# An encoder's attention heads as one straight program: value products in three f32r passes, another order of ScalarE's and TensorE's steps, scalings on GpSimd

## The chip, the core and the metric

The kernel runs on one core of one Trainium2 chip. The metric is the device time of one execution in microseconds; lower is better.

## What is computed

Two layers of an encoder over 1024 tokens of width 1024. The first mixes with a short gated convolution, the second with multi-head attention over low-rank latents; each is followed by a mixture of 64 experts. The change touches the attention heads alone. Of the reference this is the part:

```python
q = (q_lat @ w_q_up).reshape(b, s, N_HEADS, QK_HEAD_DIM)          # 8 heads, 128 + 64 dims
kv = (kv_lat @ w_kv_up).reshape(b, s, N_HEADS, QK_NOPE_DIM + V_HEAD_DIM)
k_nope, v = kv[..., :QK_NOPE_DIM], kv[..., QK_NOPE_DIM:]
k = concatenate([k_nope, k_rope for every head])
q = rms_norm(q, q_head_norm)
k = rms_norm(k, k_head_norm)
# rope on the last 64 dims of q and k
scores = einsum('bqhd,bkhd->bhqk', qb, k) * scale
probs = softmax(scores, axis=-1)
out = einsum('bhqk,bkhd->bqhd', probs, v)
```

## The kernel before, in words

The program is written engine by engine, each with its own instruction stream; what runs when is set by the order of each stream and by semaphores, with no scheduler between. The phases follow one another: convolution, experts of layer 0, attention, experts of layer 1.

In the attention phase a **tile** is 128 tokens, so a head has NT = 8 tiles, and a **step** s is one tile of queries of one head, 64 steps in all. Two kinds of work are interleaved: step s of a head, and the preparation of tile s + 8, that is of the same tile of the next head.

Preparation of a tile p: `up` (TensorE, L1937 and L1940) multiplies the latents with the head's weights into PSUM bank 4. `squares` (ScalarE, L1616, L1618) sums squares and L1620 copies all 448 columns to `raw`. `find_var` (DVE, L1789, L1792), the power -1/2 (GpSimd, L1548) and `norm_rows` (DVE) follow: L1802 to L1808 scale the rope part of q, the rest of q, k and the shared rope part of k; L1811 to L1815 rotate q. `turn_qk` (TensorE, L1947) turns the four 128x128 pieces into bank 5 or 6, and `split_qk` (DVE, L1825 to L1835) applies the gains and writes a high and a low f32r part of q and of k. GpSimd copies the value columns to `v` (L1553).

Step s: `score` (TensorE, L1959 and L1961) makes 128 x 1024 scores in ten f32r passes of 512 columns: high by high, high by low, low by high, and two for the rope part. `find_max` (DVE, L1839, L1842), `exp` (ScalarE, L1625), `invert` (DVE, L1847), `divide` (ScalarE, L1631). `turn_probs` (TensorE, L1974) turns the probabilities in two groups of four into banks 5 and 6, `copy_probs` (ScalarE, L1639, two instructions) copies them to `probsT`. Each two steps form a pair: `weigh` (TensorE, L1985) multiplies eight tiles of `v` with 256 columns of `probsT`, in plain f32 (each product is two instructions in the trace), and `copy_out` (ScalarE, L1645) stores the 256 columns.

TensorE's order in a step before is `score(s)`, `turn_qk(s+7)`, `up(s+8)`, in odd steps `weigh`, then `turn_probs(s-1)`; the first step of a head differs. ScalarE's is `exp`, `squares`, `divide`, `copy_probs(s-1)`, in odd steps `copy_out`. DVE's is `find_max`, `split_qk`, `invert`, `find_var`, `norm_rows`. The first head and the last are written out, the six between run in a loop of three passes with two heads each. In the last head nothing is prepared any more. SP loads the head's weights, and early in the last head those of the output projection (`sp_load`), which lie over buffers of the projections and of k.

f32r is the type in which a product of f32 values is one pass; a value held as a high and a low f32r part is multiplied in three passes, as `PARTS` says:

```python
HIGH, LOW = 0, 1
PARTS = ((HIGH, HIGH), (HIGH, LOW), (LOW, HIGH))
```

## Time and profile before

| | |
|---|---|
| median of 3 runs | 2750.97 us (2749.24 to 2751.67) |
| the profiled execution | 2754.65 us |
| its span | 2752.9 us |
| TensorE matmul busy | 2357.1 us, 86% |
| DVE, ScalarE, GpSimd busy | 769.6, 644.7, 502.2 us |
| attention heads, first scores to last product | 1329.8 to 1817.2 us |
| DMA moved | 701 MB, 255 GB/s over the span |

The span runs from the first instruction to the last; the execution's own time holds 1.75 us around it. Busy time of an engine is the union of its instructions; TensorE's matmuls are pipelined, so the time from one start to the next is what one costs, and the duration shown for one is longer. PE is TensorE's matmuls, PEld its weight loads, POOL is GpSimd, ACT is ScalarE. In slices of 69 us the DMA engines are busy to 9 tenths in both expert phases and to 0 or 1 in the attention phase.

### The profile page before, as it was taken

The page shows a single profiled execution, that of the slowest core. Times are in us where ns is not written, and L with a number is a line of the kernel's source. Part 1 is how long each engine was busy: PE and PEld are TensorE (multiplying, and loading weights), DVE is VectorE, ACT ScalarE, POOL GpSimd, SP SyncE. Part 2 cuts the span into 40 slices and gives each one's busy share as a digit, 9 for nine tenths or more (in the row PEclk, how much of TensorE's full clock was granted, in tenths as well). Part 3 has the DMA queues.
Part 4 walks back from the last instruction along what each step waited for, and adds up shares of the span by engine and source line. Part 5 has one row for each costly group of instructions (what it writes and reads, how often), then busy time and mean ns, then how long its engine had stood idle before and what let it go on. Part 6 is the DMA issues. An engine that isn't in the chain of part 4 may idle for free. (4 is left out here: it accounts for less than half of the span.)

```text
span 2752.9 us, 35712 instructions
## 1 busy us (share of the span) xinstructions
PE 2357.1 (86%) x12046; PEld 1438.4 (52%) x12046; DVE 769.6 (28%) x2177; ACT 644.7 (23%) x1336; POOL 502.2 (18%) x763
## 2 busy tenths in 40 slices
PE   7999996888888888878899999999598888888883
PEld 5888782333333333357688888768233333333331
DVE  4222342000000000055766666434210000000003
ACT  3111321111111111133455555542111111111111
POOL 2222211212221121211111111011122212222120
PEclk9999997999999999989999999999799999999996
DMA  4111219999999999960000000101899999999997
GB/s 120 48 54 31 77 70 367 423 424 423 423 421 419 418 417 423 389 247 1 9 9 17 8 8 0 61 16 42 355 422 423 424 424 422 422 419 422 416 388 284
DMA packets 136760, 701.17 MB, mean 255 GB/s; under 512 B 36192, under 2 KB 65888, under 8 KB 87536
## 3 DMA queue, kind: packets, MB, share of 16 engines
q1 hardware_dynamic: 116208, 666.65, 59.3%
q0 software_dynamic: 20480, 33.64, 3.2%
q8 instruction: 36, 0.59, 0.1%
q14 instruction: 36, 0.29, 0.0%
HBM read 687.59 MB, written 46.14 MB: 267 GB/s over the span
## 5 line engine op out<-in xcount | busy, mean ns | idle before, releaser
L1337 PE MATMUL ps<-arena 128*64 128x512 f32 x1536 | 445.7, 724 | 207.7 <-issue 109.9
L1318 PE MATMUL ps<-arena 128*64 128x384 f32 x2048 | 348.6, 494 | 2.1 <-DVE arena L1222 2.1
L1337 PEld LDWEIGHTS ps<-arena 128*64 128x64 f32 x1536 | 127.2, 160 | 419.4 <-issue 359.5
L1318 PE MATMUL ps<-gate_up,arena 128*64 128x384 f32 x2048 | 344.4, 489 | 0.0
L1222 DVE TENSOR_TENSOR arena<-ps,xw 128x512 f32<-128x512 f32 x128 | 88.5, 692 | 685.8 <-PE ps L1308 685.8
L843 PE MATMUL ps<-hT_split,w_split 128*128 128x512 f32 x1152 | 265.3, 392 | 3.1 <-DVE hT_split L317 3.1
L843 PEld LDWEIGHTS ps<-hT_split,w_split 128*128 128x128 f32 x1152 | 217.4, 189 | 49.1 <-DVE hT_split L317 3.9
L1231 DVE TENSOR_TENSOR arena<-arena,ps 128x192 f32<-128x192 f32 x128 | 45.4, 354 | 692.5 <-ACT arena L1128 692.5
L1133 ACT ACTIVATE arena<-ps 128x512 f32<-128x512 f32 x128 | 76.5, 597 | 675.8 <-PE ps L1337 665.8
L1318 PEld LDWEIGHTS ps<-arena 128*64 128x64 f32 x2048 | 143.3, 138 | 173.4 <-issue 166.2
L1318 PEld LDWEIGHTS ps<-gate_up,arena 128*64 128x64 f32 x2048 | 141.8, 137 | 168.4 <-issue 159.2
L1122 ACT ACTIVATE arena<-ps 128x384 f32<-128x384 f32 x128 | 62.9, 491 | 628.5 <-PE ps L1318 628.5
L1081 POOL COPY col_idx<-scatter_idx 128x1 int32 (+1 forms) x128 | 23.4, 183 | 956.6 <-ACT arena L1133 896.9
L1074 POOL DMA_INDIRECT arena<-h_rows,col_idx x128 | 134.8, 1053 | 115.6 <-POOL col_idx L1071 108.5
L1084 POOL DMA_INDIRECT y_rows<-arena,col_idx x128 | 131.8, 1030 | 112.9 <-POOL col_idx L1081 112.9
L1985 PE MATMUL ps<-arena 128*128 128x256 f32 x512 | 121.1, 391 | 7.3 <-ACT arena L1639 7.3
L1308 PEld LDWEIGHTS ps<-ident,arena 128*128 128x128 f32 x512 | 71.8, 209 | 100.7 <-issue 100.7
L1328 PEld LDWEIGHTS ps<-ident,arena 128*128 128x128 f32 x384 | 54.8, 202 | 121.0 <-issue 120.1
L1308 PE MATMUL ps<-ident,arena 128*128 128x128 f32 x512 | 96.5, 312 | 25.1 <-DMA arena<-h_rows,col_idx 25.1
L1959 PE MATMUL ps<-k_split,q_split 128*128 128x512 f32 x384 | 114.2, 406 | 0.0
L1985 PEld LDWEIGHTS ps<-arena 128*128 128x128 f32 x512 | 100.4, 197 | 23.3 <-issue 8.7
L1548 POOL TENSOR_TENSOR turned<-turned,minus_half 128x2 f32<-128x2 f32 x64 | 44.6, 698 | 354.7 <-ACT rows L1620 308.7
(218 smaller groups left out, 2926.5 us busy)
## 6 DMA issues: line engine op xcount, KB each, us to landing
arena<-in_exp_w_down SPq DMA_DIRECT2D x128, 1536.0 KB, 19.9
arena<-in_exp_w_gate SPq DMA_DIRECT2D x64, 1536.0 KB, 17.9
arena<-in_exp_w_up SPq DMA_DIRECT2D x64, 1536.0 KB, 26.1
gate_up<-in_exp_w_gate SPq DMA_DIRECT2D x64, 1536.0 KB, 18.5
gate_up<-in_exp_w_up SPq DMA_DIRECT2D x64, 1536.0 KB, 27.0
arena<-in_conv_w_in SPq DMA_DIRECT2D x24, 512.0 KB, 3.8
arena<-y_rows SPq DMA_DIRECT2D x12, 1024.0 KB, 8.2
h_rows<-rows SPq DMA_DIRECT2D x16, 512.0 KB, 2.6
```

Of the source, the lines that this page charges most:

```text
L843: last = pe.matmul(c.ps[:, 3 * h + j, :], w_split[:, j, a, k, :], hT_split[:, b, k, h * BANK:(h + 1) * BANK], start=(k == 0 and a == b), s ...
L1074: pool.indirect_dma_start(gathered[:, slot, :], None, h_halves, bass.IndirectOffsetOnAxis(ap=col_idx[:, slot, :], axis=0), bounds_check=2 ...
L1084: pool.indirect_dma_start(y_halves, bass.IndirectOffsetOnAxis(ap=col_idx[:, 2 + slot, :], axis=0), y[:, slot, :], None, bounds_check=4 * S ...
L1122: act.activation(gate_up[:, slot, :], c.ps[:, 2 + slot, 0:FF], ACT.Copy).then_inc(gate_up_copied, 1)
L1133: act.activation(y[:, slot, :], c.ps[:, 6 + slot, :], ACT.Copy).then_inc(y_copied, 1)
L1222: dve.tensor_tensor(xT[:, slot, :, :, :].rearrange("p j h m -> p (j h) m"), c.ps[:, slot, :].rearrange("p (a m) -> p a m", m=RANKS), bc(c. ...
L1308: last_ = pe.transpose(c.ps[:, slot, j * P:(j + 1) * P], rows[:, j, :], c.ident[:, :])
L1318: last_ = pe.matmul(c.ps[row:row + RANKS, 2 + slot, 0:FF], xT[:, slot, j, half, :], w_gate_up[w_slot][:, i, (4 * half + j) * FF:(4 * half ...
L1328: last_ = pe.transpose(c.ps[:, 4 + slot, j * P:(j + 1) * P], rows[:, j, :], c.ident[:, :])
L1337: last_ = pe.matmul(c.ps[half * RANKS:(half + 1) * RANKS, 6 + slot, :], hidden[:, slot, j, :], w_down[:, slot, j, half * BANK:(half + 1) * ...
L1959: pe.matmul(out, q_split[:, a, 0, q], k_split[:, par, 2 * b, keys], start=(n == 0), stop=False)
L1985: last = pe.matmul(c.ps[:, 7, 0:2 * P], v[:, par, kt, :], probsT[:, j % 2, kt, :], start=(kt == 0), stop=(kt == NT - 1))
```

## The change

1. All 64 steps are written out on every engine; the loops are gone. Slots and buffers come from the step's number.
2. `v` becomes `v_split` and `probsT` a pair of high and low parts, all f32r. GpSimd writes the high part of v with a copy and the low part with a subtraction. ScalarE writes the high part of the turned probabilities (`high_probs`), DVE the low part from the same bank (`low_probs`). `probsT` has one buffer where it had two. `weigh` becomes 24 f32r passes, in two halves of 12, the first (banks' group 0) at the end of an even step, the second after the scores of the odd step.
3. GpSimd scales the rows (L1802 to L1808 before); DVE keeps the rotation (`rotate`), one step later than the variance.
4. The gain of q is multiplied into that of k once; `split_qk` copies q's high part and makes its low part with one instruction.
5. Projections run nine tiles ahead, transposes of q and k eight. TensorE's order is `score(s)`, in odd steps the second half of `weigh`, `turn_probs(s-1)`, `up(s+9)`, in even steps the first half of `weigh`, `turn_qk(s+8)`, always into bank 5.
6. ScalarE: in odd steps `exp(s)`, `copy_out`, `high_probs(s-1)`; in even steps `high_probs(s-1)`, `exp(s)`; then `squares(s+9)`, `divide(s)`.
7. SP waits for the scores of the seventh head too before it loads the output projection's weights. The first scores of a head wait for its k tiles in two halves.

The diff, cut to its core:

```diff
-    v = piece(2, NT, VD)
-    probsT = piece(2, NT, 2 * P)
+    v_split = c.typed("v_split", v_at, [P, 2, 2, NT, VD], F32R)
+    probsT = c.typed("probsT", v_at + 4 * NT * VD, [P, 2, NT, 2 * P], F32R)
...
-    PROB_BANKS = ((5, 6), (6, 5))
+    PROB_BANKS = (5, 6)
+    TILES = NH * NT
+    AHEAD_UP, AHEAD_TURN = NT + 1, NT
...
+            def head_tile(p):
...
+                pool.tensor_tensor(head_rstd[:, slot, :], head_var[:, slot, :], c.minus_half[:, 0:2],
+                                   ALU.pow).then_inc(head_rstd_ready, 1)
+                pool.wait_ge(raw_copied, p + 1)
+                pool.wait_ge(head_rstd_ready, p + 1)
+                wait(pool, qk_turned, p - 1)
+                q_row, k_row, k_rot = (q_k_rows[:, slot, j, :] for j in (0, 2, 3))
+                wait(pool, rot_step, 3 * (p - 1))
+                pool.tensor_scalar(rot[:, 2 + slot, :], raw[:, slot, NOPE:QD], head_rstd[:, slot, 0:1], None,
+                                   ALU.mult).then_inc(rope_scaled, 1)
+                pool.tensor_scalar(q_row, raw[:, slot, 0:NOPE], head_rstd[:, slot, 0:1], None, ALU.mult)
+                pool.tensor_scalar(k_row, raw[:, slot, QD:QD + NOPE], head_rstd[:, slot, 1:2], None, ALU.mult)
+                pool.tensor_scalar(k_rot.rearrange("p (a m) -> p a m", a=2), bc(k_rope[:, i, :], 1, 2),
+                                   head_rstd[:, slot, 1:2], None, ALU.mult).then_inc(rows_scaled, 1)
                 if i == 0:
                     wait(pool, pair_products, 4 * (h - 1))
-                    pool.sem_inc(heads_begun, 1)
-                pool.tensor_copy(v[:, par, i, :], raw[:, i % 2, QD + NOPE:]).then_inc(v_copied, 1)
+                pool.tensor_copy(high, value).then_inc(v_high_ready, 1)
+                pool.wait_ge(v_high_ready, p + 1)
+                pool.tensor_tensor(v_split[:, LOW, h % 2, i, :], value, high, ALU.subtract).then_inc(v_copied, 1)
...
+            for s in range(TILES):
+                if s % 2 == 1:
+                    exp(s)
+                    if s > 1:
+                        copy_out(s // 2 - 1)
+                    high_probs(s - 1)
+                else:
+                    if s > 0:
+                        high_probs(s - 1)
+                    exp(s)
+                if s + AHEAD_UP < TILES:
+                    squares(s + AHEAD_UP)
+                divide(s)
...
-                dve.tensor_tensor(q_high, turned[:, 0:2, :], bc(qk_gain[:, 0:2], 2, P), ALU.mult).then_inc(qk_high_ready, 1)
+                dve.tensor_copy(q_high, turned[:, 0:2, :]).then_inc(qk_high_ready, 1)
...
-                for j in range(2):
-                    dve.scalar_tensor_tensor(out=q_split[:, LOW, j, cols], in0=turned[:, j, :], scalar=qk_gain[:, j:j + 1],
-                                             in1=q_high[:, j, :], op0=ALU.mult, op1=ALU.subtract)
+                dve.tensor_tensor(q_split[:, LOW, :, cols], turned[:, 0:2, :], q_high, ALU.subtract)
...
+            def low_probs(s, g):
+                dve.wait_ge(p_high_ready[g], s + 1)
+                out = slice((s % 2) * P, (s % 2 + 1) * P)
+                dve.tensor_tensor(probsT[:, LOW, 4 * g:4 * g + 4, out],
+                                  c.ps[:, PROB_BANKS[g], :].rearrange("p (a m) -> p a m", m=P),
+                                  probsT[:, HIGH, 4 * g:4 * g + 4, out], ALU.subtract).then_inc(p_low_ready[g], 1)
...
+            for s in range(TILES):
+                find_max(s)
+                if s % 2 == 1:
+                    if s + AHEAD_TURN < TILES:
+                        rotate(s + AHEAD_TURN)
+                    invert(s)
+                    low_probs(s - 1, 0)
+                    low_probs(s - 1, 1)
...
+                if s + AHEAD_TURN < TILES:
+                    split_qk(s + AHEAD_TURN, 5)
+                if s + AHEAD_UP < TILES:
+                    find_var(s + AHEAD_UP)
...
+                for kt in range(4 * part, 4 * part + 4):
+                    for a, b in PARTS:
+                        last = pe.matmul(c.ps[:, 7, 0:2 * P], v_split[:, a, q // 4 % 2, kt, :], probsT[:, b, kt, :],
+                                         start=(kt == 0 and a == b), stop=(kt == NT - 1 and a == LOW))
...
+            for s in range(TILES):
+                score(s)
+                if s % 2 == 1 and s > 1:
+                    weigh(s // 2 - 1, 1)
+                if s > 0:
+                    turn_probs(s - 1, min(s + AHEAD_TURN - 1 + 1, TILES))
+                if s + AHEAD_UP < TILES:
+                    up(s + AHEAD_UP)
+                if s % 2 == 0 and s > 0:
+                    weigh(s // 2 - 1, 0)
+                if s + AHEAD_TURN < TILES:
+                    wait(pe, p_low_ready[0], s)
+                    turn_qk(s + AHEAD_TURN, 5)
```

TensorE's instructions in one pair of steps within the heads, before. Rows stand as issued; `arena` with 256 columns x8 is `weigh`, `arena` with 192 and 256 is `up`, `ident,rows` x8 is `turn_probs`, x4 is `turn_qk`.

```order
L1985 MATMUL ps<-arena 128x256 x8
L1974 MATMUL ps<-ident,rows 128x128 x8
L1959 MATMUL ps<-k_split,q_split 128x512 x3
...
L1961 MATMUL ps<-k_split,q_split 128x512 x2
L1947 MATMUL ps<-ident,rows 128x128 x4
L1937 MATMUL ps<-arena 128x192 x3
L1940 MATMUL ps<-arena 128x256 x2
L1974 MATMUL ps<-ident,rows 128x128 x8
```

The same place with the change: an odd step from its scores on, and the even step after it.

```order
L1957 MATMUL ps<-k_split,q_split 128x512 x2
L1979 MATMUL ps<-probsT,v_split 128x256 x12
L1968 MATMUL ps<-ident,rows 128x128 x8
L1931 MATMUL ps<-arena 128x192 x3
L1934 MATMUL ps<-arena 128x256 x2
L1942 MATMUL ps<-ident,rows 128x128 x4
L1955 MATMUL ps<-k_split,q_split 128x512 x3
...
L1968 MATMUL ps<-ident,rows 128x128 x8
L1931 MATMUL ps<-arena 128x192 x3
L1934 MATMUL ps<-arena 128x256 x2
L1979 MATMUL ps<-probsT,v_split 128x256 x12
```

The transposes of q and k have moved from behind the scores to the end of the step, the transposes of the probabilities from its end to behind the scores, and the value products stand in two places.

ScalarE with the change, an odd step and the even one after it (L1640 is the exponential, L1659 `copy_out`, L1653 `high_probs`, L1630 to L1634 `squares`, L1646 `divide`):

```order
L1640 ACTIVATE rows,turned<-ps,turned 128x1024
L1659 ACTIVATE hT<-ps 128x256
L1653 ACTIVATE probsT<-ps 128x4x128 x2
L1630 ACTIVATE turned<-ps 128x192
L1632 ACTIVATE turned<-ps 128x128
L1634 ACTIVATE rows<-ps 128x448
L1646 ACTIVATE rows<-rows,turned 128x1024
L1653 ACTIVATE probsT<-ps 128x4x128 x2
L1640 ACTIVATE rows,turned<-ps,turned 128x1024
```

Before, the two copies (L1639) stood behind the division in every step; now they stand ahead of the projections' squares, behind the exponential in odd steps and ahead of it in even ones.

## Rows read from the trace of the kernel before

**Rows 1.** Windows: length, busy (instructions) of PE, PEld, DVE, ACT, POOL, clock, DMA, GB/s.

```profile
1397.61:1458.73 61.12, 58.84 (x322) 50.54 (x321) 40.74 (x153) 35.58 (x85) 7.54 (x16) 1.00 0.04 10
...
1582.37:1644.85 62.48, 58.99 (x322) 50.52 (x320) 41.35 (x155) 36.15 (x86) 7.55 (x16) 1.00 0.03 9
...
1764.66:1817.23 52.57, 44.41 (x205) 36.21 (x203) 10.86 (x22) 27.21 (x44) 0.00 (x0) 0.90 0.01 3
```

**Rows 2.** Waits from 1330 to 1780 us: in total, times, longest.

```profile
PE ps L1974 <- DVE k_split L1835: 18.6, 25, 1.5
...
PEld ps L1947 <- DVE rows L1815: 7.5, 18, 0.4
```

**Rows 3.** Timeline of PE, one pair of steps: start, us, what, count [idle before].

```profile
1412.98 3.62 PE L1985 MATMUL ps<-arena 128*128 128x256 f32 x16
1416.44 1.04 PE L1974 MATMUL ps<-ident,rows 128*128 128x128 f32 x8
1417.23 0.94 PE L1959 MATMUL ps<-k_split,q_split 128*128 128x512 f32 x3
...
1419.61 0.60 PE L1947 MATMUL ps<-ident,rows 128*128 128x128 f32 x4
...
1421.89 0.60 PE L1974 MATMUL ps<-ident,rows 128*128 128x128 f32 x4
1423.11 0.63 PE L1974 MATMUL ps<-ident,rows 128*128 128x128 f32 x4 [0.63 <-DVE k_split L1835]
...
1428.37 0.59 PE L1985 MATMUL ps<-arena 128*128 128x256 f32 x2
```

**Rows 4.** Timelines of PE and PEld, and line L329 (min/median/max ns).

```profile
1260.63 0.46 PE L1916 MATMUL ps<-w_lat_high,hT_tile_split 128*128 128x320 f32 x2
1260.92 0.31 PE L1916 MATMUL ps<-w_lat_low,hT_tile_split 128*128 128x320 f32 x1
...
324.60 1.86 PEld L329 LDWEIGHTS ps<-w_router,turned 128*128 128x128 f32 x16
...
L329 PEld LDWEIGHTS ps<-w_router,turned x256: 186/192/192, 324.6 to 1930.6; 128*128 128x128 f32 x128
```

**Rows 5.** Timeline of DVE in the same pair, and L1717 among the groups by line.

```profile
1415.25 0.26 DVE L1802 TENSOR_SCALAR arena<-rows,turned 128x64 f32<-128x64 f32 x1 [0.91 <-POOL turned L1548]
...
1416.13 0.19 DVE L1811 TENSOR_TENSOR arena<-arena,turned 128x32 f32<-128x32 f32 x1
...
1416.59 0.29 DVE L1815 TENSOR_TENSOR rows<-arena 128x128 f32<-128x128 f32 x1
1419.81 1.23 DVE L1839 TENSOR_REDUCE turned<-ps 128x1 f32<-128x1024 f32 x1 [2.93 <-PE ps L1961]
...
1421.14 0.41 DVE L1825 TENSOR_TENSOR q_split<-ps,attn_gain 128x256 fp32r<-128x256 f32 x1
...
L1717 DVE TENSOR_TENSOR hT_tile_split<-ps,hT_tile_split 128x512 fp32r<-128x512 f32 x16 | 10.4, 687 | 13.6 <-ACT hT_tile_split L1571 13.6
```

**Rows 6.** Groups by line on ACT, 1200 to 1800 us: busy, mean ns | idle before.

```profile
L1625 ACT ACTIVATE rows<-ps,turned 128x1024 f32<-128x1024 f32 x62 | 69.1, 1115 | 134.1 <-DVE turned L1842 134.1
...
L1639 ACT ACTIVATE arena<-ps 128x512 f32<-128x512 f32 x122 | 66.9, 604 | 48.1 <-PE ps L1974 48.1
...
L1645 ACT ACTIVATE hT<-ps 128x256 f32 (+1 forms) x30 | 11.7, 389 | 0.0
```

**Rows 7.** Groups by line and shape on POOL, the whole span.

```profile
L713 POOL TENSOR_TENSOR w_split<-arena,w_split 128x1024 fp32r<-128x1024 f32 x24 | 57.4, 2395 | 185.7 <-ACT w_split L740 185.7
L1548 POOL TENSOR_TENSOR turned<-turned,minus_half 128x2 f32<-128x2 f32 x64 | 44.6, 698 | 354.7 <-ACT rows L1620 308.7 <-DVE turned L1792 46.0
...
L1553 POOL COPY arena<-rows 128x128 f32<-128x128 f32 x64 | 18.7, 292 | 57.0 <-PE ps L1985 57.0
```

**Rows 8.** Line L803 on DVE: duration ns min/median/max, first and last start.

```profile
L803 DVE SCALAR_TENSOR_TENSOR rows<-rows,arena x8: 1285/3204/3206, 70.2 to 298.6; 128x1024 f32<-128x1024 f32 x8
```

**Rows 9.** Timeline of PE in the last head.

```profile
1776.76 5.38 PE L1985 MATMUL ps<-arena 128*128 128x256 f32 x16 [2.11 <-ACT arena L1639]
```

More of the change, by code:

```diff
@@ L1564, in _ @@
+                high = v_split[:, HIGH, h % 2, i, :]
+                pool.tensor_copy(high, value).then_inc(v_high_ready, 1)
+                pool.wait_ge(v_high_ready, p + 1)
+                pool.tensor_tensor(v_split[:, LOW, h % 2, i, :], value, high, ALU.subtract).then_inc(v_copied, 1)
+            for p in range(TILES):
+                head_tile(p)
             out_projection.pool_program(pool)
@@ L1664, in _ @@
-            for p in range(NT):
-                squares(p, p % 2)
-            for i in range(NT):
-                step(0, i, 0, first=True)
-            with act.Fori(0, (LAST - 1) // 2) as pair:
-                h = pair * 2 + 1
-                for par in (1, 0):
-                    for i in range(NT):
-                        step(h + (1 - par), i, par)
-            for i in range(NT):
-                step(LAST, i, 1, ends=True)
-            n = NH * NT
-            copy_probs(n - 1, NT - 1, 4 * NH - 1)
@@ new lines, in _ @@
+            for p in range(AHEAD_UP):
+                squares(p)
+            for s in range(TILES):
[11 more added lines that the diff above has]
+                divide(s)
@@ L1868, in _ @@
-            for p in range(NT):
-                find_var(p, p % 2, p)
-                if p >= 1:
-                    split_qk(p - 1, 0, p - 1, 5 + (p - 1) % 2)
-                norm_rows(p, p % 2, p)
-            for i in range(NT):
-                step(0, i, 0, first=True)
-            with dve.Fori(0, (LAST - 1) // 2) as pair:
-                h = pair * 2 + 1
-                for par in (1, 0):
-                    for i in range(NT):
-                        step(h + (1 - par), i, par)
@@ L1883, in _ @@
+            for g in range(2):
+                low_probs(TILES - 1, g)
             dve.wait_ge(router_loaded, 16 * 4)
@@ L2021, in _, with weigh @@
-            for p in range(NT):
-                pe.wait_ge(latT_ready, 2 * p + 2)
-                up(p, 0, p, 0)
+            def weigh(q, part):
+                if part == 0:
+                    pe.wait_ge(v_copied, NT * (q // 4 + 1))
+                    wait(pe, pair_copied, q)
+                pe.wait_ge(p_low_ready[part], 2 * q + 2)
+                for kt in range(4 * part, 4 * part + 4):
+                    for a, b in PARTS:
+                        last = pe.matmul(c.ps[:, 7, 0:2 * P], v_split[:, a, q // 4 % 2, kt, :], probsT[:, b, kt, :],
+                                         start=(kt == 0 and a == b), stop=(kt == NT - 1 and a == LOW))
+                last.then_inc((half_products, pair_products)[part], 1)
@@ L2024, in _ @@
+            for p in range(AHEAD_UP):
+                if p < NT:
+                    pe.wait_ge(latT_ready, 2 * p + 2)
+                up(p)
                 if p == 0:
```

244 lines of the change are left out of this document (88 added, 156 removed).

## The prediction

> **What bounds the kernel now.** I read the windows by stage first. They show that the attention heads are a stretch in which TensorE is busy 58.84 of 61.12 us a head (four pairs of steps, in the even heads of the loop) at full clock, with the other engines at two thirds or less and almost no DMA [rows 1]. The output projection and the second layer's experts only start when it is done, and no load of theirs but that of the projection's weights, early in the last head, runs beside it; so what the heads gain or lose, the whole kernel gains or loses. The same table shows 62.48 us for a head that ends a pass of the loop (1.36 us more), and the last head, where nothing is projected any more, at 52.57 us with a granted clock of 0.90. The waits of TensorE come next: the largest is for DVE's split of q and k at L1835, before the second half of the transposes of the probabilities, 25 times, 18.6 us, and the weight loader stands up to 0.4 us for the normed rows of L1815 [rows 2]. Then the timeline of one pair of steps on TensorE [rows 3], where I take every piece from start to start: value products 1412.98 to 1416.44, 3.46 us; eight transposes 0.79; ten score passes 2.38; transposes of q and k plus the projections of the next head 2.28 (1419.61 to 1421.89); then four transposes at 1421.89, which need 0.4, and the other four only at 1423.11, so 0.8 us of waiting; a second step like the first; the pair is over at 1428.37, 15.39 us. So the heads are TensorE's own work plus about 1 us of waiting a pair.
>
> **Value products (the largest edit).** Before: eight products of 256 columns in plain f32, 16 instructions a pair in 3.46 us, 0.216 us each, which is 0.422 ns a column and pass with two passes an instruction [rows 3]. Now: 24 one-pass f32r instructions of 256 columns. No row has one of 256. The nearest has 320: two of them in 0.29 us (1260.63 to 1260.92), 0.146 us each, where 320 columns at 0.422 ns are 0.135; so an f32r pass costs about 12 ns above its columns, and I take 0.108 + 0.012 = 0.120 us [rows 4]. 24 of them are 2.88 us, **0.57 us less a pair**. Lower end: no extra, 0.108 us, 2.59 us. Upper end: as long as a weight load by itself is shown, 0.19 us, 4.6 us; but the router's 16 loads under passes of only 72 columns, each shown as 0.192 us, take 1.86 us together, (1.86 - 0.19) / 15 = 0.111 us from one to the next [rows 4]; loads overlap, and I stay with 0.120. The Trainium skill ("TensorE: Matmul & The Clock Gate", section "Wait — 56ns, not 53.3ns?") has a warm matmul start every N/2.4 GHz plus about 2.5 ns, whatever its type. By that rule 24 passes take 2.6 us and the heads gain some 8 us more than I say; the f32 rows agree with it, the f32r rows of 320 columns do not, and the rows decide.
>
> **Order on TensorE.** Transposes of the probabilities now come ahead of the projections, transposes of q and k at the end of a step, value products in two halves. The split of q and k then lies under the score passes of the next step (2.38 us against a split that before took from 1421.14 to the release at 1423.11, under 2 us [rows 3, 5]). The 0.8 us of waiting goes, and with it the 0.2 us or so a pair for the rows, which are now ready a step earlier. **Gain 1.0 us a pair.**
>
> **The wait that is new.** Transposes of q and k write bank 5 and so wait for DVE's low part of the probabilities of the step before. In an odd step, counted from the last score pass: DVE starts its maximum 0.20 us later (1419.61 to 1419.81), has handed over 1.4 us after that (its next large instruction starts at 1421.14), ScalarE's exponential takes 1.12, the copy of the sums 0.39, the first high half 0.60, DVE's low half 0.69 [rows 5, 6]: 4.4 us. TensorE has half of the value products (1.44), eight transposes (0.79) and the projections (1.84) in between, 4.1 us. With the hand-overs that is a wait of **0.4 us in every odd step**. In an even step the high half goes ahead of the exponential, and the low half is done by about 2.5 us, with no wait. So a pair: 15.39 - 0.57 - 1.0 + 0.4 = 14.2 us.
>
> **At each head's first step** there are two more. The scores' second half wants the k tile that was turned just before: turned, split (some 1.7 us, since one gain goes out of it) and handed over, it comes about 0.8 us after the first half's 1.15 us. And GpSimd's first value tile of a head waits until the head before last has been weighed, which now is two steps later, holding the next tile's power behind it on its queue (it waited there before too, but with nothing behind it that the current step wanted); I take 0.65 us. So a head is 4 x 14.2 + 1.45 = 58.3 us against 61.12: **2.8 us a head**, 19.6 us over the seven heads that project.
>
> **DVE.** Four scalings of rows go to GpSimd (from 1415.25 to 1416.13, 0.9 us a step), one split instruction of two goes; four low halves a pair come, 2.8 us [rows 5]. Its load stays about two thirds of TensorE's span; costed in the chain above, nothing besides. **GpSimd** gets four scalings, a cast and a subtraction a tile. Copies of 128 columns take 0.29 us, the power 0.70, a subtraction of 1024 columns 2.40, thus about 0.3 to 0.45 for 128 [rows 7]; no row shows a scaling there. Between 2.2 us and, at twice that, 4.5 us a tile, in a step of 7.1 us and with a whole step between the projection and the use: nothing, as long as it stays under a step. **ScalarE** has the same instructions in another order. **SP** gets one wait, for the scores of the seventh head, which are there within a step. **The loops** go on every engine: twice 1.36 us, 2.8 us. Straight code loads more instructions; no row shows what that costs, and between nothing and the same 2.8 us again I take nothing, since the first head was straight code before. **Start:** nine tiles are projected ahead for eight, but one fewer projection stands before the first scores; nothing. **Last head:** the gaps of 2.1 us before the value products become two shorter ones; before, three products there took 5.38 us each for 3.62 at the lower clock (1.2 GHz in part) [rows 3, 9]. Nothing on balance, with 5 us of gain if the clock stays up, 2 us of loss from the low halves in the chain if not.
>
> **Sum.** 19.6 + 2.8 = 22 us. The profiled execution took 2754.65 us, so 2732 to 2733 in its terms; the median of the runs shown is 2750.97, 3.7 us below it, and 22 off that is **2729 us**. Lower ends together (0.108 us a pass, of which the chain of the odd step gives back a part, 6 us; the last head's 5): 2718.
>
> **Rivals.**
> (A) *Weight loads set the pace of the value products.* 24 loads for 16, each under a pass half as long. At 0.19 us a pass the pair is 1.1 us longer in the products instead of 0.57 shorter: 14.2 + 1.7 = 15.9 us, a head 65 us, 7 x 3.9 - 2.8, and the kernel about 25 us **slower, 2775**. It decides from 0.149 us a pass on (22 us over 32 x 24 passes above 0.120). For it: loads are shown as 0.19 us. Against: the router's start every 0.111 us [rows 4].
> (B) *DVE and GpSimd get in each other's way.* DVE's sum at L803 takes 1.285 us alone and 3.204 where GpSimd subtracts at the same time [rows 8]. The rotation (four instructions with two operands in SBUF, 0.75 us) and the low halves would be stretched so while GpSimd works on the next tile; with 0.7 us more in both chains of a pair (half of what the rotation could be stretched by, once a step) the gain falls to about 3 us, 2748. That is a rule of the skill too ("GPSIMD Engine Reference", section "Key points": contention with Vector instructions that have two SBUF inputs); the trace agrees for instructions of 1024 columns and shows none for short ones. Against: DVE idles a third of the time, and the power of 0.70 us runs beside it already.
> (C) *The order gives nothing.* The 1.0 us of waiting turns up elsewhere in the ring of score, maximum, exponential, division, transposes. Then only 32 x 0.57 and the loops are left, less 1.45 a head: 18 + 2.8 - 10, 11 us, 2740.
>
> **Chances.** Forecast 0.63, with its own range 2718 to 2736; A 0.10; B 0.12; C 0.15. The range has to take in C and B and leaves A and the tail below out: 2717 to 2748. A measurement of this kernel can tell about 0.2% (5.5 us) from no change. Faster: the forecast, C and a little of B, 0.80. Same: most of B, 0.09. Slower: A and a worse B, 0.11.
>
> **What would show it.** Value products at about 0.12 us from start to start, 1.44 us a half; pairs of 14.2 us, with a longer third and fourth; no wait of transposes on L1835's successor but one of the q and k transposes on the low halves, about 0.4 us in odd steps; heads of 58 us; 22 us less before the output projection and nothing after it. Wrong it is if passes start 0.15 us apart or more, if the rotation takes over 1 us, or if DVE waits for GpSimd's scaling in every step.

## The result, and the profile after

The changed kernel takes **2728.88 us** in the median of four runs (2726.91 to 2731.35), the kernel before beside it 2751.32 us (2749.24 to 2754.48): a ratio of 0.9919, 95% interval 0.9907 to 0.993. The forecast was 2729, and the outcome is the likeliest case of the prediction. The profiled execution took 2731.35 us, 23.3 less than the one before:

| stretch | before | after | difference |
|---|---|---|---|
| up to the end of the latents | 1280.3 | 1279.8 | -0.5 |
| start: to the first scores | 49.5 | 53.2 | +3.7 |
| first scores to last product | 487.4 | 464.7 | -22.7 |
| output projection and experts | 935.7 | 931.9 | -3.8 |

The last row is code that the change doesn't touch, and it varies by itself: 931.9 us here and 934.3 in the second trace of the same kernel (run 1), 931.1 to 935.1 over all traces with the new heads. The windows of the trace (columns as in [rows 1]) show the start, two heads, and the last head in two parts:

```profile
1279.80:1332.98 53.18, 29.96 (x135) 24.62 (x133) 26.72 (x103) 13.12 (x53) 30.80 (x59) 0.78 0.04 11
1455.10:1513.67 58.57, 56.21 (x355) 50.12 (x353) 44.05 (x129) 35.94 (x85) 29.19 (x56) 1.00 0.04 11
1513.67:1572.20 58.53, 56.17 (x355) 50.05 (x353) 44.03 (x128) 35.88 (x85) 29.14 (x56) 1.00 0.03 10
...
1689.26:1747.66 58.40, 52.88 (x335) 46.84 (x333) 43.57 (x125) 34.63 (x80) 26.21 (x51) 1.00 0.16 57
1747.66:1797.70 50.04, 41.81 (x254) 36.49 (x254) 21.44 (x39) 26.69 (x44) 0.00 (x0) 0.93 0.05 20
```

A head is 58.55 us for 61.12 and 62.48 [rows 1], every head alike now, and GpSimd (fifth engine column) is busy 29 us in it for 7.5. The last stretch is 50.04 us for 52.57, at a granted clock of 0.93 for 0.90. A plain pair on TensorE (timeline: start, duration, line, count, idle before):

```profile
1426.09 1.78 PE L1979 MATMUL ps<-probsT,v_split 128*128 128x256 f32 x12
1427.70 0.60 PE L1942 MATMUL ps<-ident,rows 128*128 128x128 f32 x4
1428.06 0.94 PE L1955 MATMUL ps<-k_split,q_split 128*128 128x512 f32 x3
...
1430.44 1.60 PE L1979 MATMUL ps<-probsT,v_split 128*128 128x256 f32 x12
1431.87 1.04 PE L1968 MATMUL ps<-ident,rows 128*128 128x128 f32 x8
1432.74 1.14 PE L1931 MATMUL ps<-arena 128*128 128x192 f32 x6
1433.72 1.03 PE L1934 MATMUL ps<-arena 128*128 128x256 f32 x4
1434.83 0.66 PE L1942 MATMUL ps<-ident,rows 128*128 128x128 f32 x4
...
1438.51 1.14 PE L1931 MATMUL ps<-arena 128*128 128x192 f32 x6
1439.48 1.03 PE L1934 MATMUL ps<-arena 128*128 128x256 f32 x4
1440.16 1.06 PE L1979 MATMUL ps<-probsT,v_split 128*128 128x256 f32 x6
```

The pair is 14.07 us (1426.09 to 1440.16) for 15.39 [rows 3]. Twelve f32r passes take 1.43 us (1430.44 to 1431.87), 0.119 each. From the projection's second part to the transposes of q and k it is 1.11 us (1433.72 to 1434.83); the four products need 0.86 of it, so 0.25 us is a wait. The waits from 1320 to 1790 us (total, times, longest), against [rows 2]:

```profile
POOL v_split L1573 <- PE ps L1979: 37.8, 6, 6.3
...
PEld ps L1942 <- DVE probsT L1837: 24.8, 28, 2.2
...
PE ps L1942 <- POOL rows L1567: 9.1, 6, 1.5
...
PE ps L1955 <- DVE k_split L1823: 5.3, 8, 1.2
```

The 18.6 us for the split before the transposes of the probabilities are gone. The transposes of q and k (L1942) wait for DVE's low half (L1837) in every odd step, and at the second step of six heads for GpSimd's rows; the first scores of a head (L1955) wait for the k tile's split. GpSimd at such a head's beginning:

```profile
1454.19 0.60 POOL L1567 TENSOR_SCALAR rows<-turned 128x128 f32<-128x128 f32 x1
1461.11 0.29 POOL L1573 CAST v_split<-rows 128x128 fp32r<-128x128 f32 x1 [6.31 <-PE ps L1979]
1461.49 0.46 POOL L1575 TENSOR_TENSOR v_split<-rows,v_split 128x128 fp32r<-128x128 f32 x1
1461.91 0.72 POOL L1556 TENSOR_TENSOR turned<-turned,minus_half 128x2 f32<-128x2 f32 x1
...
1464.53 0.60 POOL L1567 TENSOR_SCALAR rows<-turned 128x128 f32<-128x128 f32 x1
```

It stands 6.31 us before the cast of the head's first value tile, and the next tile's rows, due behind it, come at 1465.1; TensorE's transposes start at 1465.28, after 1.52 us of idling.

### The profile page after: what moved, and what is told of

The parts are those of the page before. It is cut to its first block and busy times, and to the rows that moved or that the text cites. A ratio compares the mean times of both kernels' runs of the same rounds, so it can differ in the third digit from the quotient of the medians.

```text
span 2729.6 us, 35801 instructions
## 1 busy us (share of the span) xinstructions
PE 2336.9 (86%) x12300; PEld 1437.3 (53%) x12302; DVE 794.8 (29%) x1986; ACT 645.8 (24%) x1336; POOL 674.7 (25%) x1083
## 5 line engine op out<-in xcount | busy, mean ns | idle before, releaser
L1955 PE MATMUL ps<-k_split,q_split 128*128 128x512 f32 x384 | 115.9, 410 | 5.3 <-DVE k_split L1823 5.3
L1979 PE MATMUL ps<-probsT,v_split 128*128 128x256 f32 x768 | 109.6, 293 | 5.6 <-DVE probsT L1837 5.6
L1979 PEld LDWEIGHTS ps<-probsT,v_split 128*128 128x128 f32 x768 | 102.3, 194 | 10.4 <-issue 6.6
L713 POOL TENSOR_TENSOR w_split<-arena,w_split 128x1024 fp32r<-128x1024 f32 x24 | 57.4, 2395 | 185.8 <-ACT w_split L740 185.8
```

The source lines that it names most:

```text
L1955: pe.matmul(out, q_split[:, a, 0, q], k_split[:, h % 2, 2 * b, keys], start=(n == 0), stop=False)
L1979: last = pe.matmul(c.ps[:, 7, 0:2 * P], v_split[:, a, q // 4 % 2, kt, :], probsT[:, b, kt, :], start=(kt == 0 and a == b), stop=(kt == NT ...
```

## Experiments

Twelve kernels ran, each an edit of the changed kernel unless it says otherwise. All ratios are against the kernel before on the same chip. Differences between runs in microseconds are of medians, in part from different chips, on which the kernel before took 2750.9 to 2753.2 us; what is said of heads, pairs and starts is read from one trace of each kernel.

**1. The change again.**

> The changed kernel once more, untouched, as the measure for the others of this group. 0.992 of the kernel before, 2729 us, whichever theory holds; pairs of steps of 14.07, 14.07, 14.9 and 15.5 us in a head of 58.5.

2728.96 us (2724.93 to 2730.35), 0.991 (0.9895 to 0.9924). It reproduces, and shows what varies: from the first tile's projection to the first scores it is 50.3 us here (1280.57 to 1330.86) and 52.6 in the first profile of the change. The six products of 192 columns, 1.14 us at full clock (2.4 GHz) and 2.13 at half (1.2 GHz), tell why:

```profile
1302.43 1.30 PE L1931 MATMUL ps<-arena 128*128 128x192 f32 x6
...
1308.20 2.08 PE L1931 MATMUL ps<-arena 128*128 128x192 f32 x6
...
1313.50 1.14 PE L1931 MATMUL ps<-arena 128*128 128x192 f32 x6
...
1317.86 1.14 PE L1931 MATMUL ps<-arena 128*128 128x192 f32 x6
```

A tile is 4.36 us at full clock (1313.50 to 1317.86) and 5.3 to 6.6 where the clock is at half for part of it. Of the executions with the order of the change's own start, the profiled ones of runs 2, 4, 5 and 8 have one such tile and need 48.0 us, this one has three, the first profile and run 6 have four (52.6 and 52.5). Differences of up to 4.6 us between two traces are that; below, starts and heads are told apart for it.

**2. Value products in plain f32.**

```diff
-                    for a, b in PARTS:
-                        last = pe.matmul(..., v_split[:, a, q // 4 % 2, kt, :], probsT[:, b, kt, :], ...)
+                    last = pe.matmul(..., v[:, q // 4 % 2, kt, :], probsT[:, kt, :], ...)
```

with `low_probs` and the low value tile gone, and every wait for a low half turned into one for the high half.

> The changed kernel with its value products in plain f32 again (8 products of 256 columns a pair in place of 24 f32r passes), so DVE has no low halves to make and GpSimd only copies the value tile; the order of the work is kept. My theory: the products take 0.57 us a pair longer (3.46 for 2.88), but the wait of the q and k transposes in odd steps goes, since they now wait for ScalarE's high half alone; in the trace of the change that wait is about 0.25 us of TensorE and the second half-step is otherwise full. So pairs of 14.07 + 0.57 - 0.25 = 14.4 us, about 28 x 0.32 = 9 us slower than the change, plus some 3 in the last head: 2741, 0.996 of before. Rival 1, the passes are worth their full 0.57 a pair and DVE's low halves cost nothing (something else would hold TensorE in the odd step): 16 to 18 us slower, 2746. Rival 2, the low halves cost as much as the passes save (DVE's 2.8 us a pair also delays the split or the maximum): same as the change within 3 us.

2730.74 us, 0.9922 (0.991 to 0.9934): **in this order the f32r passes, the prediction's largest edit, are worth 1.8 us** in the median, which the two intervals don't separate from nothing. The window of one head, starts of the value products as its ends:

```profile
1406.31:1465.78 59.47, 57.89 (x322) 50.63 (x321) 34.66 (x112) 35.91 (x86) 25.12 (x48) 1.00 0.04 10
```

A plain pair is 14.34 us for 14.06, so 0.28 slower and not 0.57: the wait for the low half is gone with the low half, as my theory had it, and seven heads lose 6.4 us. The total is nearer to Rival 2, for two reasons outside the pairs: its start is 2.3 us shorter by the clock (48.0 for 50.3), which is no merit of the edit, and the last head's pairs, which have no projections to cover a low half, take 10.74 us for 11.15. From the first scores to the last product it takes 465.06 us for 462.06, so with equal starts the passes are worth 3 to 4 us. The fourth pair of a head hides them too: it is 15.5 us with either, since GpSimd's rows hold it.

**3. The scalings back on DVE.**

```diff
             def rotate(p):
+                dve.wait_ge(raw_copied, p + 1)
+                dve.wait_ge(head_rstd_ready, p + 1)
+                dve.tensor_scalar(rot[:, 2 + slot, :], raw[:, slot, NOPE:QD], ...)
...
```

> The changed kernel with the four scalings of a tile (2.2 us on GpSimd, 0.9 on DVE in the trace of before) back on DVE, ahead of its rotation; the rest untouched. My theory: in the heads DVE stands idle 0.5 us ahead of the low halves of an odd step and 0.5 us more ahead of them after its reciprocal, so 0.9 us more is covered there, and the heads stay at 58.5 within 0.5; the first scores, which came at 1332.98 for 1329.8 before, come 3 to 4 us earlier again, since a tile of the start no longer goes through GpSimd's 2.2 us; so 3 to 4 us faster than the change, 2725. Also the wait of the q and k transposes on GpSimd's rows at a head's second step (1.5 us, six times) shrinks, since the stalled value tile no longer holds the next tile's rows: up to 1.3 us a head, 2717 to 2725. Rival, what the prediction set at nothing is worth something: the 0.9 us lie in the chain from maximum to the low half of an odd step, q and k transposes wait 0.4 us longer in each of 28 pairs, 7 to 11 us slower than the change, 2738.

2746.21 us, 0.9976 (0.9968 to 0.9985): 17 us slower than the change. My theory was right for the heads, which stay within 0.5 us (plain pairs 14.06, a head 58.75), and the rival fell, since odd steps wait no longer than before. But no time is gained: the wait at a head's second step doesn't shrink (that pair is 15.68 us for 15.47), since the power still stands behind the stalled value tile, and the start, where I expected 3 to 4 us of gain, loses most of the time: 61.9 us from the first projection to the first scores (1281.84 to 1343.77) for 50.3, or 48.0 at best. Rows of its timeline, all engines:

```profile
1303.37 2.13 PE L1932 MATMUL ps<-arena 128*128 128x192 f32 x6
1305.29 1.20 PE L1935 MATMUL ps<-arena 128*128 128x256 f32 x4
...
1307.44 0.17 DVE L1785 TENSOR_SCALAR turned<-turned 128x2 f32<-128x2 f32 x1
1307.55 0.25 DVE L1795 TENSOR_SCALAR arena<-rows,turned 128x64 f32<-128x64 f32 x1
...
1308.76 0.29 DVE L1807 TENSOR_TENSOR rows<-arena 128x128 f32<-128x128 f32 x1
...
1309.15 1.09 PE L1943 MATMUL ps<-ident,rows 128*128 128x128 f32 x4 [2.66 <-DVE rows L1807]
...
1310.03 2.13 PE L1932 MATMUL ps<-arena 128*128 128x192 f32 x6
```

DVE takes the new tile's variance (L1785) first, which waits for that tile's projection and its squares, and only then the scalings and the rotation of the tile before; TensorE waits for these and projects no further tile. One turn is 6.66 us. Six products of 192 columns take 2.13 us, where they take 1.14 at full clock: TensorE idles 2.66 us of each turn, and in each of seven tiles running it was back at 1.2 GHz when it began, and near 2.4 GHz again in the tile's last products (1.05 to 1.39 us for 1.03); the granted clock over the last six of these turns is 0.75. In the change the scalings run on GpSimd beside the ring, a turn is 4.36 us with 1.89 of idling, and after one to four tiles the clock stays up. My estimate from these rows: the 0.75 us of scalings make a turn of 5.1 us at full clock, and products and transposes at half clock (0.99 + 0.17 + 0.46) the other 1.6, 6.7 in all. No run gave this start another clock, so the split between the two is not tested.

**4. The copy of the sums behind the high halves.**

```diff
                     exp(s)
-                    if s > 1:
-                        copy_out(s // 2 - 1)
                     high_probs(s - 1)
+                    if s > 1:
+                        copy_out(s // 2 - 1)
```

> The changed kernel with one move on ScalarE: in odd steps the copy of a pair's sums (0.38 us) comes behind the two high halves instead of between the exponential and them. My theory: this copy is in the chain that the q and k transposes wait for in an odd step (exponential, copy, high half, DVE's low half), they wait about 0.25 us there, so the wait goes in 28 pairs: 7 us faster than the change, 2722, pairs of 13.8 us. Rival: the q and k transposes are not held by this chain but by the score chain (TensorE is then simply a step behind its own scores, and what is gained comes back as a wait of the next transposes of the probabilities for the division): 2729, pairs stay at 14.07.

2720.50 us, 0.9886 (0.9873 to 0.9899): 8.5 us faster than the change. Its timeline in an odd step:

```profile
1427.38 1.08 ACT L1653 ACTIVATE probsT<-ps 128x512 fp32r<-128x512 f32 x2
1427.90 1.03 PE L1934 MATMUL ps<-arena 128*128 128x256 f32 x4
1428.00 1.29 DVE L1837 TENSOR_TENSOR probsT<-ps,probsT 128x512 fp32r<-128x512 f32 x2 [0.26 <-ACT probsT L1653]
1428.33 0.39 ACT L1659 ACTIVATE hT<-ps 128x256 f32<-128x256 f32 x1
1428.77 0.63 PE L1942 MATMUL ps<-ident,rows 128*128 128x128 f32 x4
```

From the projection's second part to the transposes it is 0.87 us now, so nothing waits, and pairs are 13.79 us, a head 57.72. My theory holds: seven heads give 5.8 us, the shorter start of this execution (48.0) 2.3.

**5. The copies ahead of the exponential.** This undoes one part of the change.

```diff
-                    exp(s)
                     if s > 1:
                         copy_out(s // 2 - 1)
-                    high_probs(s - 1)
+                    exp(s)
```

with `high_probs(s - 1)` ahead of both.

> The changed kernel with one part undone: in odd steps ScalarE makes the two high halves and the copy of the sums first and the exponential behind them. The change's description puts the exponential first. By the trace of the change, with copies first the low half is ready 1.5 us earlier, before the projections end, so the wait of the q and k transposes in odd steps (0.25 us) goes as it did with the copy moved behind; the exponential comes 1.9 us later (from 1433.9 in the pair of 1426), its squares 0.35 us later, the division would end at 1437.4, just before the next transposes of the probabilities at 1437.6. My theory: as copy_out_last, 0.988 to 0.990 of before, 2720 to 2725. Rival, the order of the change is right: the division comes 0.3 us or more too late in each odd step, 2730 or above. If it equals the change, both effects cancel.

2752.5 us, 1.0002 (0.9992 to 1.0013): the whole gain is gone, against my theory. A plain pair is 15.11 us; only the fourth of a head, which GpSimd holds, stays at 15.45. The rows that say why:

```profile
1445.09 1.09 ACT L1653 ACTIVATE probsT<-ps 128x512 fp32r<-128x512 f32 x2 [3.88 <-PE ps L1968]
...
1446.33 1.13 ACT L1640 ACTIVATE rows<-ps,turned 128x1024 f32<-128x1024 f32 x1
...
1447.65 0.16 DVE L1843 RECIPROCAL turned<-turned 128x1 f32<-128x1 f32 x1 [2.19 <-ACT rows L1640]
1447.73 1.27 DVE L1837 TENSOR_TENSOR probsT<-ps,probsT 128x512 fp32r<-128x512 f32 x2
...
1448.45 0.66 PE L1942 MATMUL ps<-ident,rows 128*128 128x128 f32 x4 [1.12 <-DVE probsT L1837]
```

The high halves are early, but DVE's queue has the reciprocal ahead of the low halves, and it waits 2.19 us for the exponential. I had looked at ScalarE's order and not at DVE's.

**6. The same, with DVE's low halves ahead of the reciprocal.**

```diff
-                    invert(s)
                     low_probs(s - 1, 0)
                     low_probs(s - 1, 1)
+                    invert(s)
```

> As the run with the copies ahead of the exponential in odd steps, and in addition on DVE the two low halves ahead of the reciprocal in odd steps. In that run DVE's reciprocal stood ahead of the low halves on its queue and waited for the exponential until 1447.5, the low halves came behind it and TensorE waited 1.1 us. My theory: it was this pairing that cost 23 us, not the place of the exponential; with both moved the low half is ready before the projections end and the division as early as in the change (squares of the next tile hold it, not the exponential): pairs of 13.8 us, as with the copy moved behind, 2720 to 2723. Rival: the exponential has to be first in any case (the division comes later and the next transposes of the probabilities wait): 2730 to 2750.

2728.13 us, 0.9912 (0.9896 to 0.9928), the change's time. The pairs are what I expected, 13.77 us, and a window of one shows TensorE busy throughout:

```profile
1410.48:1424.25 13.77, 13.77 (x90) 12.63 (x89) 11.06 (x33) 8.86 (x22) 7.24 (x15) 1.00 0.00 0
```

So the pairing of two orders cost the 23 us of run 5. What keeps this run from 2720 is elsewhere: its start was one of four slow tiles (52.5 us), and in the last head, where no projection covers the later division, the transposes of the probabilities wait 1.19 us for it instead of 0.42, the clock falls for two of the value products (twelve passes 2.77 and 2.90 us for 1.67), and pairs are 11.9 to 13.9 us for 11.15. In the heads that project, then, either order gives the same pairs or better ones; by this trace the exponential is better first only in the last head, and a kernel with each order in its place was not run.

**7. The kernel before, loops written out.**

```diff
-            with pe.Fori(0, (LAST - 1) // 2) as pair:
+            for pair in range(0, (LAST - 1) // 2):
```

and so for the other engines.

> The kernel before with one part of the change alone: the loops over pairs of heads of all five engines written out straight, nothing else. The prediction's term: the end of a loop pass costs 1.36 us twice (62.48 for 61.12 us a head), so 2.8 us faster, 0.999 of before. Rival 1: the loop's end costs more than the heads show, since each engine's own branch (waits and registers inside the loop too) also slows the steps: 5 us or more, 0.998. Rival 2: straight code has to be fetched, as much is given back: 1.000 within 0.0005.

2750.82 us, 0.9997 (0.9988 to 1.0006). In its trace all heads are alike:

```profile
1457.67:1519.04 61.37, 58.75 (x321) 50.58 (x320) 40.67 (x153) 35.51 (x85) 7.53 (x16) 1.00 0.03 10
```

The loop's end is gone, but a head is 61.37 for the 61.12 of a head inside the loop: 1.4 us less over six heads, not 2.8. The interval holds both my value and none; the two traces' heads favour about half of it. The straight code loads 0.77 MB of instructions on one queue for 0.59; whether that is what makes the steps longer was not tested.

**8. The first value tile of a head later on GpSimd's queue.**

```diff
             for p in range(TILES):
                 head_tile(p)
+                if p % NT == 1:
+                    value_tile(p - 1)
+                if p % NT > 0:
+                    value_tile(p)
```

where `value_tile` is the cast and subtraction taken out of `head_tile`.

> The changed kernel with one move on GpSimd's queue: at a head's first tile the value tile is made behind the scalings of the second tile, instead of before its power, so the wait for the products of the head before last (6.3 us, six times) holds nothing that the current step wants. My theory: the wait of the q and k transposes for GpSimd's rows (1.5 us of TensorE at the second step of six heads) goes and nothing takes its place: 6 x 1.4 = 8 us faster than the change, 2721, fourth pair of a head 14.1 for 15.45. Rival: the third tile's projection or its squares wait for the late value tile (two buffers of raw rows), and the time comes back as a wait of the projections: 2725 to 2729.

2717.98 us, 0.9877 (0.9861 to 0.9892): 11 us faster than the change. The fourth pair is 14.06 us for 15.47 and a head 57.13, 1.42 less, as my theory had it (six heads, 8.5 us); 2.3 of the 11 are the shorter start of 48.0.

**9. The rotation ahead of the variance in the start.**

```diff
-                find_var(p)
                 if p >= 1:
                     rotate(p - 1)
+                find_var(p)
```

> The changed kernel with one move on DVE in the start (nine tiles before the first scores): the rotation of the tile before comes ahead of the new tile's variance, which waits for that tile's projection and squares. In the trace of the change the start is a ring: projection, squares, variance, rotation of the tile before, transposes, next projection, 4.36 us a tile at full clock and 5.7 to 6.2 where TensorE is at half clock, while in the run with the scalings on DVE all nine tiles stood at half clock, 6.7 us each. My theory: the ring is what bounds the start; out of it, a tile takes what GpSimd needs, 3.7 us, 0.65 x 8 = 5 us faster than the change, 2724, and the first scores at 1325 or before. Rival: GpSimd's chain (power, four scalings, then the rotation) bounds the start already: first scores at 1330 to 1333 as now, 2729.

2722.64 us, 0.9893 (0.9878 to 0.9908): 6.3 us faster. The start is 44.2 us (1281.31 to 1325.55), 3.7 below the best of the change, and a tile takes 3.97 us, 0.39 less. The ring was the bound, as my theory had it, though a tile takes 3.97 and not 3.7 us, and run 3 had seven slow tiles and not nine. What TensorE waits for next is GpSimd's scaled rows:

```profile
1309.26 0.63 PE L1942 MATMUL ps<-ident,rows 128*128 128x128 f32 x4 [1.51 <-POOL rows L1567]
...
1313.24 0.63 PE L1942 MATMUL ps<-ident,rows 128*128 128x128 f32 x4 [1.50 <-POOL rows L1567]
```

All four runs with this start (9 to 12) had one slow tile only.

**10. Runs 4, 8 and 9 together.**

> The changed kernel with the three moves that helped alone: the copy of the sums behind the high halves in odd steps, the first value tile of a head behind the second tile's scalings, the rotation ahead of the new variance in the start. They sit in three different places (a wait in odd steps, one at a head's second step, the start), so my theory is that they add: by the places in their traces 6.3 + 8.6 + 5.6 = 20 us off 2729, 2709; pairs of 13.8, 13.8, 14.7 and 13.8 us, a head of 56.2. Rival: two of them hide the same wait (the fourth pair waits on DVE's low half once GpSimd no longer holds it), 2715 or more.

**2705.07 us, 0.9834** (0.982 to 0.9847), 24 us faster than the change: the start is 44.0 us for 50.3, and of the seven heads that project six give 2.5 us each and the last 0.8, which is 22 us in the traces. The fourth pair is 13.79 us, so no second wait stood behind the first, and the three gains add. One head:

```profile
1386.67:1442.69 56.02, 55.42 (x354) 50.07 (x353) 44.09 (x129) 35.92 (x85) 28.89 (x56) 1.00 0.04 11
```

**11. Run 10 with plain f32 value products.**

> The three moves, with the value products in plain f32 (no low halves on DVE, no low value tile on GpSimd). In the order of the change this edit cost 0.28 us a pair only, since the low halves brought a wait with them, and the whole came to 1.8 us. My theory: where the wait of the q and k transposes is gone, the f32r passes are worth their full 0.57 us a pair: pairs of 14.34 for 13.79, heads 2.2 us longer, 15 us over the seven heads, less 1 to 4 that the last head and the start give back: 11 to 15 us slower than the kernel with the three moves, about 2721. Rival: they are worth little here too, because DVE's 2.8 us a pair cost elsewhere: within 4 us of it.

2717.42 us, 0.9879 (0.9864 to 0.9894): 12.4 us slower than run 10; plain pairs 14.34 us for 13.79 and a head 58.2 for 56.0. In the traces 10.7 us lie between the first scores and the last product, the start is 2.0 us shorter (42.0 for 44.0, GpSimd's subtraction being gone), and 3.4 us of the difference lie behind the heads, in code that neither kernel touches. So the same edit is worth 3.0 us between first scores and last product in run 2 and 10.7 here. Two waits make the difference: in the change's order the passes bring the wait of the odd step with them, and the fourth pair, held by GpSimd, hides what they save.

**12. Run 10 with the q part of the projection between a head's first score halves.**

```diff
                     if s % NT == 0:
+                        if half == 1 and s + AHEAD_UP < TILES:
+                            up(s + AHEAD_UP, "q")
                         pe.wait_ge(qkT_ready, s + 4 * (half + 1))
```

> The kernel with the three moves, and a fourth on TensorE: at each head's first step the q part of the next tile's projection (six products of 192 columns, 0.98 us) comes between the two halves of the scores, whose second half waits for the split of the k tile just turned. In the trace with three moves the pair with that step takes 14.66 us for 13.80. My theory: the wait is covered, the pair takes 13.85 us, eight times 0.8 us less, about 6 us off 2705: 2699, 0.981 of before. Rival: the maximum, the exponential and the division of that step all come up to 0.1 us later than with the bare wait and their ring has no slack there, or the projection's bank is not yet read out (it then waits for ScalarE's raw copy of the tile before): 2703 or more.

2705.98 us, 0.9834 (0.9821 to 0.9848): nothing that the medians show, and neither mechanism that I wrote down. The third pair is 14.61 us for 14.66, where I expected 13.85, the fourth 13.68 for 13.79. The wait for the split is covered, but the value products behind now wait for the low half, as too little is left between them and the transposes of the probabilities:

```profile
1440.29 1.03 PE L1944 MATMUL ps<-arena 128*128 128x256 f32 x4
1441.77 1.67 PE L1991 MATMUL ps<-probsT,v_split 128*128 128x256 f32 x12 [0.46 <-DVE probsT L1844]
```

## Why the prediction was right, and where its steps were not

**The heads.** 58.3 us forecast, 58.55 measured; plain pairs 14.2 and 14.07. The pass of 256 columns was taken at 0.120 us and took 0.119. The Trainium skill's rule ("TensorE: Matmul & The Clock Gate", section "Wait — 56ns, not 53.3ns?") would have given 0.109; the trace disagrees with it here as it did at 320 columns. The section names no type, so "whatever its type" is how the prediction read it. The wait of the odd step was put at 0.4 us and was 0.25. The chain behind it was right, and taking the copy of 0.39 us out of it took the wait away (run 4). The longer third pair was put at 0.8 us and was 0.87 (1440.16 to 1455.10, less 14.07). The fourth was put at 0.65 and was 1.4: the right stall, but I had counted too little of what GpSimd still has to do for the next tile once it is free, a power and four scalings, 3.2 us (1461.91 to 1465.1). Run 8 is the proof of the place.

**What the order gives and what the passes give.** The sum had 0.57 us a pair for the passes and, as a term of its own, 0.4 for the wait that they cause. Runs 2 and 11 show that these two terms belong together: 0.28 net in this order, 0.55 where the wait is gone. "The largest edit", as the prediction called it, was one of the smallest in time. The 1.0 us a pair that the prediction gave to the order of TensorE is the main gain: with plain products, in run 2, a pair is still 14.34 us for 15.39 before, and run 3 shows that the place of the scalings adds nothing to it. Rival C, in which the order gives nothing, would have been 2740. The gain does rest on more than TensorE's order: run 5 moved three instructions of ScalarE and lost all of it.

**GpSimd's scalings.** The scalings, the cast and the subtraction were put at 2.2 to 4.5 us a tile, from copies of 0.29. They take 3.0: a scaling 0.61 for 128 columns and 0.45 for 64, the subtraction 0.46, the cast 0.29:

```profile
L1565 POOL TENSOR_SCALAR rows<-rows,turned 128x128 f32<-128x128 f32 x48 | 29.2, 609 | 0.0
...
L1575 POOL TENSOR_TENSOR v_split<-rows,v_split 128x128 fp32r<-128x128 f32 x48 | 22.1, 461 | 4.1
L1563 POOL TENSOR_SCALAR arena<-rows,turned 128x64 f32<-128x64 f32 x48 | 21.7, 452 | 7.7 <-POOL turned L1556 6.7 <-issue 1.0
...
L1806 DVE TENSOR_TENSOR rows<-arena 128x128 f32<-128x128 f32 x48 | 18.3, 382 | 1.7
```

"Nothing, as long as it stays under a step" held for plain pairs: run 3 leaves them at 14.06. In the start their place is worth a lot: there the rotation behind the new variance closes a ring, and on DVE the scalings lie in it: 61.9 us for 48.0 to 52.6. Rival B is there, and small: the last addition of the rotation (L1806) takes 382 ns in the mean for 292 [rows 5]. It is 291 to 294 where it runs beside nothing on GpSimd or beside the power, and up to 412 beside a scaling; 0.09 us a step in place of the 0.7 of the rival. That agrees in direction with the Trainium skill ("GPSIMD Engine Reference", section "Key points"), which has such pairs contend.

**The start** was costed at nothing. From the first projection to the first scores it was 48.95 us before (47.8 in run 7), and is 48.0 to 52.6 in the change (run 1); the profiled execution has the worst of these and lost 3.7 us. The step that failed is "nine tiles are projected ahead for eight, but one fewer projection stands before the first scores". Nine stand there in both kernels, and I counted TensorE's work, while the start is a ring over four engines, in which TensorE idles and its clock is at half for one to four tiles. The kernel before has such a ring too, of 4.31 us a tile for 4.36, so at full clock nothing is nearly right; what the term left out is the clock, and that the ring can be shortened. Run 9 shows the ring, since one move on DVE shortens it.

**The last head**: nothing on balance, with 5 of gain if the clock stays up. It gained 2.5 us (50.04 for 52.57). From one pair's products to the next it took 12.10, 13.85, 13.85 and 9.08 us before, and takes 11.15 four times now: the twelve passes stay at full clock (1.67 us), where three products took 5.38 us for 3.62 before [rows 9]. So the first three gain 6.3 us. The end gives 3.8 back: the fourth is 2.1 us longer, since the last transposes wait 2.72 us for the division, and behind it the last 24 passes take 5.46 us, all at the lower clock (0.213 us from start to start), where the last product took 3.69. **The loops**: 2.8 forecast, about 1.4 shown by the heads' windows of run 7. Its interval does not exclude either.

So the sum came out within 0.2 us, but its terms did not: the fourth pair (0.75 us, six times, too low) and the start (up to 3.7) against the wait of the odd step (0.15 us, 28 times, too high), the last head (2.5) and the 3.8 us after the heads, which no edit made: 8.2 us one way and 10.5 the other. That the number fits is partly luck; the pairs are not.

**What stays open.** What decides how many tiles of the start run at half clock was not tested; with the rotation first it was one in all four traces. Orders that keep the copies first in seven heads and the exponential first in the last one were not tried, nor was DVE's order of run 6 with the exponential left first, nor TensorE's order alone in the kernel before, so how the 1.0 us a pair divides among the orders of TensorE, ScalarE and DVE is open.

## What to carry to other kernels

Price an edit together with the wait that it causes: the same f32r passes were worth 3.0 us in the heads with their new wait and GpSimd's stall in the way, and 10.7 without. Where two engines' orders meet in one chain, read both queues: an instruction early on ScalarE is worth nothing when DVE's queue has another one ahead of its reader. After a change that gains, list the waits that are new, and look for one instruction to move in each; three such moves gave as much again as the change.

## What the runs showed of the hardware

An f32r pass of 256 columns starts every 0.119 us at full clock and every 0.213 at half (the last 24 of the change), a plain f32 product every 0.43 us for its two (8 instructions in 1.72 us, 1439.47 to 1441.19 in run 2), so three f32r passes cost 0.36 for 0.43. A scaling by a value per partition costs GpSimd 0.61 us for 128 columns and 0.45 for 64, where DVE took 0.28 and 0.26. DVE's addition of 128 columns from SBUF is stretched from 0.29 to 0.41 us by such a scaling, and not by GpSimd's power over two columns. And in a ring TensorE's clock can be down again at each turn: in run 3, with 2.66 us of idling in turns of 6.7, TensorE was at 1.2 GHz at the start of every turn, seven in a row, while in the change, with 1.89 us of idling in turns of 4.36, it came back to 2.4 GHz after one to four. No run shows what makes the difference.
